# Cross attention's value product as three products of rounded halves

## The reference

```
def memory_cross_attention(hn, mem, w_xq, w_xkv, g_mem, g_xq, g_xk, w_xo):
    q = rmsnorm((hn @ w_xq).reshape(B, T, 4, 256), g_xq)
    k, v = jnp.split(rmsnorm(mem, g_mem) @ w_xkv, 2, axis=-1)
    k = rmsnorm(k.reshape(B, M, 4, 256), g_xk)
    logits = jnp.einsum('bthd,bmhd->bhtm', q, k) * (256 ** -0.5)
    p = jax.nn.softmax(logits, axis=-1)
    o = jnp.einsum('bhtm,bmhd->bthd', p, v).reshape(B, T, D_MODEL)   # this product
    return o @ w_xo
```

## Time and profile before

| | |
|---|---|
| median of 3 runs | 1991.21 us (1989.88 to 1992.22) |
| the profiled execution's own time | 1990.7 us, of which the span is 1988.9 us |
| granted TensorE clock over the span | 0.998 |
| PE busy | 1965.5 us |
| DVE busy | 1245.8 us |
| ACT busy | 895.9 us |
| POOL busy | 903.1 us |

### The profile page before, as it was taken

The page is one execution under the profiler, slowest core; times in us unless marked ns, Lnnn a source line. Parts: engine busy times, 40 slices in busy tenths (PEclk is TensorE's granted clock), DMA queues, the critical chain, the costliest instruction groups (busy, mean ns, idle before and its releaser), DMA issues.

```text
span 1988.9 us, 32439 instructions
## 1 busy us (share of the span) xinstructions
PE 1965.5 (99%) x11614; PEld 1702.0 (86%) x11614; DVE 1245.8 (63%) x1941; ACT 895.9 (45%) x1603; POOL 903.1 (45%) x458
## 2 busy tenths in 40 slices
PE   9999899999999999999999999999999999999998
PEld 7788788878999988899998888887777888999887
DVE  4586885346788787887768773463552347877111
ACT  5234444344566522556652252225663246666322
POOL 3344323326577654544445534443224445444443
PEclk9999999999999999999999999999999999999999
DMA  6253222212333386233339634432222223333321
GB/s 211 82 156 109 79 67 83 85 33 95 106 107 105 103 314 248 98 116 106 105 108 327 243 114 142 116 95 85 67 69 87 85 96 95 107 106 106 106 96 63
DMA packets 67246, 234.71 MB, mean 118 GB/s; under 512 B 7632, under 2 KB 9040, under 8 KB 66640
## 3 DMA queue, kind: packets, MB, share of 16 engines
q1 hardware_dynamic: 66432, 232.29, 35.6%
q10 hardware_dynamic: 720, 1.15, 0.2%
HBM read 225.54 MB, written 2.10 MB: 114 GB/s over the span
## 4 chain that ended last, share of the span: by engine, by line
PE 95%; DVE 3%; ACT 1%; issue 1%; DMA 0%; POOL 0%; SPq 0%; POOLq 0%; DVEq 0%; ACTq 0%
PE bank L2268 13%; PE bank L2269 12%; PE bank L2274 12%; PE bank L2448 9%; PE bank L2447 9%; PE bank L2451 9%; PE bank L2392 5%; PE bank L2393 5%; PE bank L2398 5%; PE bank L2242 1%; PE bank L2244 1%; PE bank L2243 1%; PE bank L2566 1%; PE bank L2574 1%; PE bank L2567 1%; PE bank L2871 1%
## 5 line engine op out<-in xcount | busy, mean ns | idle before, releaser
L555 POOL TENSOR_TENSOR wlo<-raw,whi 128x1024 fp32r<-128x1024 f32 x233 | 578.8, 2485 | 804.6 <-ACT whi L674 804.3
L674 ACT ACTIVATE whi<-raw 128x1024 fp32r<-128x1024 f32 x233 | 245.9, 1057 | 473.4 <-PE bank L2398 217.3
L2268 PE MATMUL bank<-xh,whi 128*128 128x512 f32 x764 | 302.2, 396 | 0.6 <-DVE proj L1421 0.3
L2269 PE MATMUL bank<-xl,whi 128*128 128x512 f32 x764 | 297.7, 390 | 0.0
L2392 PE MATMUL bank<-hh,whi 128*128 (+1 forms) x480 | 186.9, 389 | 1.0 <-ACT whi L674 1.0
L2393 PE MATMUL bank<-hl,whi 128*128 (+1 forms) x480 | 186.8, 389 | 0.0
L2274 PE MATMUL bank<-xh,wlo 128*128 128x512 f32 x736 | 181.6, 389 | 0.0
L2268 PEld LDWEIGHTS bank<-xh,whi 128*128 128x128 f32 x764 | 143.4, 188 | 34.5 <-issue 3.9
L2269 PEld LDWEIGHTS bank<-xl,whi 128*128 128x128 f32 x764 | 143.5, 188 | 29.5 <-issue 0.7
L2274 PEld LDWEIGHTS bank<-xh,wlo 128*128 128x128 f32 x736 | 138.1, 188 | 28.9
L1744 DVE CUSTOM_DVE_ANT_0 xn<-ada_w,csilu 128x1024 f32<-128x1024 f32 x72 | 134.2, 1864 | 18.6 <-ACT csilu L787 10.1
(11 more groups left out here) (401 smaller groups left out, 4674.5 us busy)
## 6 DMA issues: line engine op xcount, KB each, us to landing
raw<-units SPq DMA_DIRECT2D x341, 512.0 KB, 3.6
ada_w<-ada_rows SPq DMA_DIRECT2D x72, 512.0 KB, 5.6
h<-x_t SPq DMA_DIRECT2D x8, 256.0 KB, 5.7
out_t<-h SPq DMA_DIRECT2D x8, 256.0 KB, 2.1
raw<-units SPq DMA_DIRECT2D x4, 256.0 KB, 5.3
mem_in<-mem_t SPq DMA_DIRECT2D x1, 1024.0 KB, 11.7
turned_q<-proj SPq DMA_DIRECT2D x4, 256.0 KB, 6.0
dec<-decays SPq DMA_DIRECT2D x4, 256.0 KB, 5.4
```

The source lines that it names most:

```text
L555: pool.tensor_tensor(wlo[:, j % 2 * UNIT:(j % 2 + 1) * UNIT], raw[:, j * UNIT:(j + 1) * UNIT], whi[:, j % 2 * UNIT:(j % 2 + 1) * UNIT].bit ...
L674: act.activation(whi[:, v % 2 * UNIT:(v % 2 + 1) * UNIT], raw[:, slot * UNIT:(slot + 1) * UNIT], ACT.Copy).then_inc(hi_ready, 1)
L2268: mm(bank[:, 0:n], wh, chunk(rhs[0], t, n), start=t == 0, stop=False)
L2269: mm(bank[:, 0:n], wh, chunk(rhs[1], t, n), start=False, stop=False)
```

## The change

- ACT's list gets two rounded copies of 128x1024, `vmem` to `vmem_hi`, after the two square roots of the memory keys' norm and before layer "out"'s own part.
- POOL's list gets two subtractions of 128x1024, `vmem - vmem_hi` to `vmem_lo` (written over `vmem`): one after the low part of unit 4 of "out", one after that of unit 5. The loop over the low parts is cut at these places.
- `pt_x` becomes a high and a low tile. ACT now rounds both banks into the high tile (two instructions for each head in place of one), DVE subtracts both (two in place of one copy), each waiting for ACT's.
- PE makes, for each `kb` and `d`, three fp32r products in place of one float32 product: for a head first the 8 that need ACT's tile, then the 4 that need DVE's. Banks 3 and 4 are free when DVE's subtractions are done; the first product waits once for POOL's two low parts.

```diff
-        p_x, pt_x = (at("p_x0", 48, 1024), at("p_x1", 56, 1024)), at("pt_x", 52, 1024)
+        p_x, pt_x = (at("p_x0", 48, 1024), at("p_x1", 56, 1024)), (at("pt_x_hi", 52, 1024, f32r), at("pt_x_lo", 60, 1024, f32r))
+        vmem_hi, vmem_lo = at("vmem_hi", 64, C * M, f32r), at("vmem_lo", 80, C * M, f32r)
...
-            low_parts(2, xo0 + 3)
+            def memory_value_lows(m):
+
+                pool.wait_ge(vmem_copied, C + m + 1)
+                cols = slice(m * D, (m + 1) * D)
+                pool.tensor_tensor(vmem_lo[:, cols], vmem[:, cols], vmem_hi[:, cols].bitcast(f32), ALU.subtract).then_inc(vmem_split, 1)
+            ahead = L["out"].u0 + 5
+            low_parts(2, ahead)
+            memory_value_lows(0)
+            low_parts(ahead, ahead + 1)
+            memory_value_lows(1)
+            low_parts(ahead + 1, xo0 + 3)
...
+            for m in range(2):
+                act.activation(vmem_hi[:, m * D:(m + 1) * D], vmem[:, m * D:(m + 1) * D], ACT.Copy).then_inc(vmem_copied, 1)
             residual_layer("out", "xattn", yh, "g_xattn")
...
-                act.activation(xat.pt[:, 0:T], banks[3][:, :], ACT.Copy).then_inc(xat.s_pt_act, 1)
+                for kb in range(2):
+                    act.activation(xat.pt[0][:, kb * T:(kb + 1) * T], banks[3 + kb][:, :], ACT.Copy).then_inc(xat.s_pt_act, 1)
...
-                dve.wait_ge(xat.s_tr, hd + 1)
-                if hd >= 1:
-                    dve.wait_ge(xat.s_pv, hd)
-                dve.tensor_copy(xat.pt[:, T:2 * T], banks[4][:, :]).then_inc(xat.s_pt_dve, 1)
+            def memory_probabilities_low(hd):
+
+                for kb in range(2):
+                    dve.wait_ge(xat.s_pt_act, 2 * hd + kb + 1)
+                    cols = slice(kb * T, (kb + 1) * T)
+                    tt(xat.pt[1][:, cols], banks[3 + kb][:, :], xat.pt[0][:, cols].bitcast(f32), ALU.subtract).then_inc(xat.s_pt_dve, 1)
...
-                bank_free[3], bank_free[4] = [(xat.s_pt_act, hd + 1)], [(xat.s_pt_dve, hd + 1)]
+                bank_free[3], bank_free[4] = [(xat.s_pt_dve, 2 * hd + 1)], [(xat.s_pt_dve, 2 * hd + 2)]
...
-                pe.wait_ge(xat.s_pt_act, hd + 1)
-                pe.wait_ge(xat.s_pt_dve, hd + 1)
-                for d in range(2):
-                    take(6 + d)
-                    o = (2 * hd + d) * P
-                    for kb in range(2):
-                        last = mm(banks[6 + d][:, :], vmem[:, kb * D + o:kb * D + o + P], xat.pt[:, kb * T:(kb + 1) * T],
-                                  start=kb == 0, stop=kb == 1)
+                if hd == 0:
+                    pe.wait_ge(vmem_split, 2)
+                for kb in range(2):
+                    pe.wait_ge(xat.s_pt_act, 2 * hd + kb + 1)
+                    for d in range(2):
+                        if kb == 0:
+                            take(6 + d)
+                        w0 = kb * D + (2 * hd + d) * P
+                        mm(banks[6 + d][:, :], vmem_hi[:, w0:w0 + P], xat.pt[0][:, kb * T:(kb + 1) * T], start=kb == 0, stop=False)
+                        mm(banks[6 + d][:, :], vmem_lo[:, w0:w0 + P], xat.pt[0][:, kb * T:(kb + 1) * T], start=False, stop=False)
+                for kb in range(2):
+                    pe.wait_ge(xat.s_pt_dve, 2 * hd + kb + 1)
+                    for d in range(2):
+                        w0 = kb * D + (2 * hd + d) * P
+                        last = mm(banks[6 + d][:, :], vmem_hi[:, w0:w0 + P], xat.pt[1][:, kb * T:(kb + 1) * T],
+                                  start=False, stop=kb == 1)
```

More of the change, by code:

```diff
@@ L287, in two_block_kernel @@
         vmem_tr, vmem_copied, gate_silu = (sem(n) for n in ("vmem_tr", "vmem_copied", "gate_silu_product_scaled"))
+        vmem_split = sem("vmem_split")
         kmem_sq, kmem_sum, kmem_root, kmem_rstd, kmem_done = (
@@ L315, in __init__ @@
                     self.s_sinkmax, self.s_sink, self.s_sum = sem("swa_sinkmax"), sem("swa_sink"), sem("swa_sum")
-                self.s_tr, self.s_pt_act, self.s_pt_dve = sem(name + "_tr"), sem(name + "_pt_act"), sem(name + "_pt_dve")
+                self.s_tr, self.s_pt_dve = sem(name + "_tr"), sem(name + "_pt_dve")
+                if name != "fox":
+                    self.s_pt_act = sem(name + "_pt_act")
                 self.s_pv, self.s_hi, self.s_lo = sem(name + "_pv"), sem(name + "_hi"), sem(name + "_lo")
@@ L562, in low_parts @@
                 a, b = -(-u // 4), end // 4
+                if a >= b:
+                    for v in range(u, end):
+                        low_part(v, v % 4)
+                    return
                 for v in range(u, 4 * a):
@@ L2042, in memory_normalise @@
                     ts(p, p, rs[:, 4 * hd + q:4 * hd + q + 1], None, ALU.mult).then_inc(xat.s_pn, 1)
-            def memory_probabilities_copy(hd):
-                dve.wait_ge(xat.s_tr, hd + 1)
-                if hd >= 1:
-                    dve.wait_ge(xat.s_pv, hd)
-                dve.tensor_copy(xat.pt[:, T:2 * T], banks[4][:, :]).then_inc(xat.s_pt_dve, 1)
+            def memory_probabilities_low(hd):
[3 more added lines that the diff above has]
+                    tt(xat.pt[1][:, cols], banks[3 + kb][:, :], xat.pt[0][:, cols].bitcast(f32), ALU.subtract).then_inc(xat.s_pt_dve, 1)
             def memory_out_low(hd):
@@ L2070, in _ @@
             memory_maxima(1)
-            memory_probabilities_copy(0)
+            memory_probabilities_low(0)
             query_variances(1)
@@ L2076, in _ @@
             memory_normalise(2)
-            memory_probabilities_copy(1)
+            memory_probabilities_low(1)
             memory_out_low(0)
@@ L2080, in _ @@
             memory_out_low(1)
-            memory_probabilities_copy(2)
+            memory_probabilities_low(2)
             memory_normalise(3)
-            memory_probabilities_copy(3)
+            memory_probabilities_low(3)
             memory_out_low(2)
```

## The result

| | kernel before | changed kernel |
|---|---|---|
| median | 1990.23 us (22 runs, 1987.88 to 1992.85) | 1993.12 us (22 runs, 1992.23 to 1994.13) |
| ratio to before | | 1.0013, interval 1.0008 to 1.0019 |
| timed again later | 1990.78 us (27 runs) | 1992.39 us (11 runs), ratio 1.0010, interval 1.0001 to 1.0019 |
| span of the profiled execution | 1988.9 us | 1991.0 us |

The intervals are 95% intervals of the ratio. The change costs 2.9 us in the first comparison (interval 1.6 to 3.8 us) and 1.6 us in the second (0.2 to 3.8).

The account below looks back on a forecast made before the run. PE was taken as the bound, busy 1965.5 of 1988.9 us with 95% of the chain. +1.7 us in "out" and -1.2 in cross attention gave +0.5 on 1991.2, so 1991.7 us, range 1988.5 to 1994.4.

Parts of the forecast that it names:

- that of the weight loads: Rival: weight loads not hidden, 0.40 us a product, +5.5 us in cross attention and +1.7 in "out", 1998.4; chance 0.04.
- PE's own work: Cross attention values: twelve fp32r products take 2.76 us for 3.43 a head, saving 0.67, at most 2.7 for four heads.
- The waits in cross attention: PE waits for DVE's `yl` 0.9 us before values 1 and 0.6 before values 3, so the stage gains 1.2 us.
- The turns in "out": DVE and POOL alternate at memory in layer "out"; `h` of chunk 4 is 4.1 us late, PE waits 1.7 at unit 6.
- The rival in which DVE keeps the ports through its four `kmem`: In "out", DVE's four products run unbroken; PE waits 0.9 us at unit 7, -0.3 in all, 1990.9; chance 0.22.
- ScalarE's two copies: ACT's two copies ahead of "out", 2.0 us together, fit in 2.71 us of idle time; cost 0.
- The sum: Whole kernel: +1.7 us in "out", -1.2 in cross attention, +0.5 in all, 1991.7 us; chance 0.45.

Follow-up runs that it names:

- both: Changed kernel with the edits of lows_in_xq and bank_first together: 1988.23 us, ratio 0.9986 to the kernel before; timed again 1988.83 us, 0.9990.
- bank_first: Changed kernel with DVE's `yl` of heads 0 and 2 put ahead of its subtractions for heads 1 and 3: 1991.38 us, ratio 1.0003 to the kernel before.
- lows_in_xq: Changed kernel with POOL's two subtractions moved from layer "out" to layer "xq": 1989.15 us, ratio 0.9994 to the kernel before; timed again 1990.34 us.
- one_in_xq: Changed kernel with only the second of POOL's two subtractions moved to layer "xq": 1990.14 us, ratio 0.9996 to the kernel before.
- after_again: Changed kernel, unaltered, run for a second trace; its end, from DVE's last addition to `h` to its last pass, took 6.28 us.
- after_timed: Changed kernel, unaltered, timed again with a third trace: 1992.39 us, ratio 1.0010 to the kernel before.

## Why the prediction was right, and where its size was off

The forecast was +0.5 us, 1991.7, in a range of 1988.5 to 1994.4; measured were 1993.12 (+2.9) and 1992.39 (+1.6). The mechanism came out as foreseen, and no case but that of the weight loads lay more than 4 us from the kernel before, so that "no change that can be told" was a safe call and says little for the sum. The sum was too small: +0.5 lies outside the interval of the first comparison and inside that of the second. That 1991.7 stands only 1.4 us from 1993.12 is in part luck, since the three runs of the kernel before that it was counted from (1991.21) lay 1.0 us above the median of 22. By its steps:

- **PE's own work.** 2.76 us for twelve products was right for a group that follows other products (2.97 for one that begins after a wait, above), and the bound of 2.7 for the whole held: "both", without the long waits, gives 2.46 us in its trace and 2.56 and 1.95 in its medians.
- **The waits in cross attention.** Foreseen were 0.9 us ahead of values 1 and 0.6 ahead of values 3 and none elsewhere; measured 1.00 and 0.64. Yet the stage won 0.65 us and not 1.2. The term that was too small is the restart: I had let the products step on at 0.23 us from the first, but the first product after a wait takes 0.47 (at 413.66 and 427.24 above). Its weight load of 0.19 us begins only 0.03 us ahead of it (413.63), that of a later product 0.23 ahead (413.97 for 414.20), so the load is not hidden here; whether this is all of the 0.24 was not tried apart. Two restarts by 0.24 are 0.48 us, and the two waits are 0.14 longer than foreseen; that is 0.62 for the missing 0.55. "bank_first" bears it out: without the two waits it gains 1.81 and not 1.64 us, although a restart after a gap of 0.14 has come ahead of values 2 (1.64 + 0.48 - 0.14 - 0.24 = 1.74).
- **The turns in "out".** `ssum` to 324.20 (325.04 less 0.83 foreseen), `kmem` held twice, `h` of chunk 4 3.95 us late where 4.1 were foreseen, the high part of unit 6 ready at 334.43, 4.2 late, PE's wait 1.9 where 1.7 were foreseen. With a restart of 0.24 that makes 2.14 of the 2.2 us that the layer lost. The rival in which DVE keeps the ports through its four `kmem` fell: 5.94 us is two waits, and it was unit 6 and not unit 7 that waited. The prediction read POOL's longer 2.73 us at 325.70 in the earlier trace rows, on which the rival rested, as a wait for the rest of the `kmem` products; but these are 0.40 us apart from 324.51, so that only the fourth, of 325.70, was left, and the row fits turns as well. `ssum` ended at 324.75, 0.55 us after POOL's. The rule cited from the Trainium skill ("SBUF — State Buffer", section "SBUF: two separate sides"), a lock for the whole instruction, agrees with that. While both engines have such work queued, the turns go instruction by instruction: four `kmem` took 5.94 us with two of POOL's operations in the way and 3.80 with one.
- **ScalarE's two copies** cost nothing, as foreseen: 2.00 us for both, and 0.82 us of idle time left of 2.71.
- **The sum.** The forecast was 1.7 - 1.2 = +0.5 us; with the measured sizes it is 2.2 - 0.65 - 0.3 = +1.25. Of this gap of 0.75, the restarts after three waits, which no term had, are 0.7, the longer waits 0.2 in "out" and 0.14 in cross attention, and the norm takes 0.3 back. The second timing (+1.6) agrees with that. The first (+2.9) is 1.6 above, and 1.25 lies just outside its interval. What made up this rest is not shown. Executions of one kernel differ by as much: the end of the kernel was 1.1 us longer than before in the first pair of traces and 0.2 in the second. But that this is chance was not shown either: none of the changed kernel's 33 runs is below 1991.75 us, while those of before reach 1987.88.
- **What cannot be settled.** Why PE's wait in the norm behind cross attention is 0.3 us shorter in every kernel with the change or its splitting (and not in the second trace of the kernel before) was not tried. Nor was it tried why the 22 runs of the changed kernel lie so close together (1992.2 to 1994.1) and those of before do not (1987.9 to 1992.9).

A version faster than both came out of it: "both", 0.9986 and 0.9990 of the kernel before.

## What to carry to other kernels

An engine that is 45% busy can still be the wrong place for a moved job: before putting an elementwise operation on GpSimd, look in the timeline for the VectorE operations with two tensors from memory that lie in its way, and count how often they meet, as two holds (1.65 and 2.13 us) were free here and a third cost 2.2 us. Where a step frees a buffer that TensorE waits for, put it ahead of steps that feed a later part of the same product; that swap was worth 1.8 us here (88.62 against 86.81 us). And when a change adds waits to a chain of matmuls, price each by its length and the restart of 0.24 us, even where the wait itself is as short as 0.14 us.

## What the runs showed of the hardware that was not expected

**The scatter of the runs has places in the trace.** At the end of the kernel PE has only small products (1-column ones, three of 512 columns, then the broadcast of the last norm, 16 of 128 columns), and its granted clock falls from 1.00 (2.4 GHz) to 0.50 (1.2 GHz) there, at a different moment in each execution. In most traces it fell ahead of the broadcast or as that began, and the end, from DVE's last addition to `h` to its last pass over `h`, took 5.53 to 6.96 us. In the first trace of "lows_in_xq" and in that of "one_in_xq" it fell only behind the broadcast, and the end took 4.8. Two stretches of the first of these, where the broadcast already runs (us, busy us of PE, PEld, DVE, ACT, POOL with counts, granted clock, DMA share, GB/s):

```profile
1978.00:1979.00 1.00, 1.00 (x11) 1.00 (x11) 0.00 (x0) 0.74 (x2) 0.00 (x0) 1.00 0.00 0
1979.00:1980.00 1.00, 0.94 (x9) 0.75 (x7) 0.92 (x2) 0.02 (x1) 0.00 (x0) 1.00 0.00 0
```

and of the changed kernel, which is still at the products ahead of it:

```profile
1978.00:1979.00 1.00, 1.00 (x7) 1.00 (x7) 0.00 (x0) 0.74 (x1) 0.00 (x0) 0.57 0.00 0
1979.00:1980.00 1.00, 1.00 (x4) 0.95 (x5) 0.00 (x0) 0.35 (x2) 0.00 (x0) 0.50 0.00 0
```

A second such place lies in the attention of the first block, at 236 to 244 us, where PE waits a good deal. In the first trace of the kernel before the clock stayed at 1.00 there; in the second it fell, and what follows came 2.1 us later than it would have (that trace was 0.4 us ahead of the first until then, and 1.7 behind it afterwards). In the changed kernel it stayed in the first trace and fell in the other two ("after_again", "after_timed"). The kernel before, first trace, then second, with the 4 us ahead of it, in which PE was busy for 2.44:

```profile
236.00:240.00 4.00, 2.69 (x22) 1.96 (x20) 4.00 (x7) 0.43 (x2) 2.35 (x1) 1.00 0.10 19
240.00:244.00 4.00, 4.00 (x38) 3.87 (x38) 2.90 (x8) 2.52 (x10) 0.00 (x0) 1.00 0.37 125
```

```profile
232.00:236.00 4.00, 2.44 (x24) 2.24 (x24) 3.13 (x7) 3.80 (x10) 0.85 (x1) 1.00 0.42 131
236.00:240.00 4.00, 3.42 (x18) 2.42 (x17) 4.00 (x7) 0.17 (x2) 2.36 (x1) 0.60 0.15 16
240.00:244.00 4.00, 4.00 (x23) 4.00 (x22) 1.54 (x5) 2.37 (x9) 0.00 (x0) 0.54 0.30 119
```

**A loop has two paces.** In the loop at 1700 to 1830 us PE is busy throughout, at full clock, and yet makes 1117 products in 130 us in one execution and 1106 in another of the same kernel, which is 11 products of 0.118 us, 1.3 us. The first and the second trace of the kernel before:

```profile
1700.00:1830.00 130.00, 130.00 (x1117) 130.00 (x1116) 102.54 (x176) 83.62 (x173) 62.88 (x40) 1.00 0.33 105
```

```profile
1700.00:1830.00 130.00, 130.00 (x1106) 130.00 (x1106) 101.96 (x172) 82.72 (x171) 62.18 (x40) 1.00 0.34 107
```

VectorE's and ScalarE's counts fall too (176 to 172, 173 to 171), so it is not a matter of missing records of PE alone. All three traces of the changed kernel have the quicker pace (1116 or 1117), so the pace does not explain why it is slower. What sets it was not found. Together these places move an execution by more than the change does, which is why single traces could not be compared by their spans here, but only stretch by stretch.
